# Two-layer encoder step on one core: the second layer's projection finishes block by block, with the sample's loads and first steps inside it

## The reference, cut to what matters

```
p = rmsnorm(x) @ w_in[l]      # -> mixer a | b | c | cross q | gate
even l: o = chunk-band softmax attention
odd  l: o, S = HGRN2 recurrence, then rmsnorm per head
y = concat(o, cross_attn(q_x, mem_k, mem_v)) * silu(gate);  x = x + y @ w_out[l]
```

```
A = cumsum(log_f)
o     = sum_s (q_t . exp(A_t - A_s) k_s) i_s  +  (q * exp(A)) @ S
S_new = exp(a_last) * S + (k * exp(a_last - A))^T @ i
```

## Time and profile before

| what | value |
|---|---|
| median of three runs | 2802.57 us (2802.24 to 2803.62) |
| the profiled execution: its own time | 2802.87 us |
| its span, first to last instruction | 2800.9 us |
| busy share of PE, PEld, DVE, ACT, POOL | 95%, 81%, 40%, 34%, 9% |
| mean granted TensorE clock | 0.973 |
| DMA | 273.21 MB, mean 98 GB/s |

### The profile page before, as it was taken

One profiled execution on the slowest core, in us unless ns is written; L12 is line 12 of the kernel. 1 busy time (PEld: TensorE's weight loads), 2 busy tenths in 40 slices (PEclk: granted clock), 3 DMA queues, 4 the chain that ended last, 5 costly groups with the idle time before them and its releaser, 6 DMA issues. The chain is left out here.

```text
span 2800.9 us, 45370 instructions
## 1 busy us (share of the span) xinstructions
PE 2651.8 (95%) x17253; PEld 2259.0 (81%) x17253; DVE 1111.9 (40%) x2432; ACT 957.4 (34%) x2314; POOL 265.5 (9%) x516
## 2 busy tenths in 40 slices
PE   7999999999669999999999999999998599999997
PEld 4899999999646777777778999999997488888886
DVE  5211111022145555555545112211122477777774
ACT  5111111111144555554545122111111545554553
POOL 2000000000002111111111000000001111111111
PEclk9999999999789999999999999999999799999999
DMA  6321212111593222221335223212112633333331
GB/s 226 141 77 64 74 66 72 69 63 63 119 263 115 71 63 77 71 84 55 95 106 143 78 89 125 99 63 78 63 62 92 221 100 95 95 104 111 95 95 59
DMA packets 271920, 273.21 MB, mean 98 GB/s; under 512 B 13808, under 2 KB 228904, under 8 KB 271764
## 3 DMA queue, kind: packets, MB, share of 16 engines
q1 hardware_dynamic: 258168, 221.43, 25.4%
q0 software_dynamic: 11936, 44.96, 4.6%
q10 hardware_dynamic: 1660, 4.75, 0.4%
HBM read 175.64 MB, written 100.18 MB: 98 GB/s over the span
## 5 line engine op out<-in xcount | busy, mean ns | idle before, releaser
L640 PE MATMUL pj_acc<-xh,pj_wh 128*128 128x384 f32 (+1 forms) x1120 | 400.4, 357 | 5.6 <-DVE pj_wl L610 5.6
L640 PE MATMUL pj_acc<-xl,pj_wh 128*128 128x384 f32 (+1 forms) x1120 | 400.6, 358 | 0.0
L640 PE MATMUL pj_acc<-xh,pj_wl 128*128 128x384 f32 (+1 forms) x1120 | 400.6, 358 | 0.0
L902 PE MATMUL pj_acc<-xl,pj_wh 128*128 128x384 f32 (+1 forms) x1040 | 371.1, 357 | 0.0
L902 PE MATMUL pj_acc<-xh,pj_wl 128*128 128x384 f32 (+1 forms) x1040 | 370.9, 357 | 0.0
L902 PE MATMUL pj_acc<-xh,pj_wh 128*128 128x384 f32 (+1 forms) x1040 | 370.5, 356 | 0.0
L640 PEld LDWEIGHTS pj_acc<-xh,pj_wh 128*128 128x128 f32 x1120 | 211.0, 188 | 24.0 <-DVE pj_wl L610 5.8
L640 PEld LDWEIGHTS pj_acc<-xh,pj_wl 128*128 128x128 f32 x1120 | 210.9, 188 | 18.3
L640 PEld LDWEIGHTS pj_acc<-xl,pj_wh 128*128 128x128 f32 x1120 | 210.9, 188 | 17.8
L1993 ACT COPY pb_pt<-pb_TP 128x384 f32<-128x384 f32 (+2 forms) x272 | 107.0, 393 | 312.1 <-PE pb_TP L1725 237.0
L902 PEld LDWEIGHTS pj_acc<-xh,pj_wl 128*128 128x128 f32 x1040 | 195.2, 188 | 16.8
(11 more groups left out here) (310 smaller groups left out, 4402.3 us busy)
## 6 DMA issues: line engine op xcount, KB each, us to landing
proj<-pj_stg SPq DMA_DIRECT2D x168, 192.0 KB, 1.9
proj<-pj_stg SPq DMA_DIRECT2D x112, 256.0 KB, 2.0
pj_wraw<-in_w_in_dram POOLq DMA_DIRECT2D x26, 1024.0 KB, 6.1
hg_x<-x_mid SPq DMA_DIRECT2D x17, 512.0 KB, 3.5
out_dram<-hg_x POOLq DMA_DIRECT2D x17, 512.0 KB, 3.0
bg_x<-in_x_prompt_dram SPq DMA_DIRECT2D x16, 512.0 KB, 4.5
pb_gate<-proj SPq DMA_DIRECT2D x16, 512.0 KB, 5.0
pb_x<-in_x_prompt_dram SPq DMA_DIRECT2D x16, 512.0 KB, 3.4
```

The lines of the kernel that those rows point to most:

```text
L640: ins = nc.tensor.matmul(acc[b][:, 0:n], w[p][:, k], x[:, k, at:at + n], start=(k == 0 and x is xh and w is wh), stop=(k == KD - 1 and x i ...
L902: ins = nc.tensor.matmul(acc[b][:, 0:n], w[p][:, k], x[:, k, at:at + n], start=(k == 0 and x is xh and w is wh), stop=(k == KD - 1 and x i ...
```

## The change

**norm_project.** Groups 26 and 27 are taken out of the loop. They are computed as a pair, block by block: block 0 of both, then block 1 of both, and so on. So block 0 of the tokens is no longer needed when a fifth of this tail is over. The tokens now lie in one buffer per block (`xh[b]`, `xl[b]`) instead of one for all. Tiles of the sample are placed over the first of these buffers: after the second store of the tail SP issues the loads of q, f, k, the values, the cross queries and the memory keys; after the fourth the memory values. The first product and the four steps (DVE and ACT parts) come between the tail's blocks. The section no longer ends with a wait for the stores; these waits stand in `sample_mix`, before the first state is stored (SP) and before `o_s` is written (DVE).

```diff
                     sweep(sp, lo, hi, 1, body)
-                for b in range(NBLK):
-                    sp.wait_ge(s_st[b], 16 * NG)
-                    sp.wait_ge(s_st2[b], 16 * MG)
+                tok = slice(SEQ, NTOK)
+                mk, mv = (c[l].rearrange("b (t p) h d -> p (b t) (h d)", p=P) for c in (cache_mem_k, cache_mem_v))
+
+                def load_sample():
+                    sp.wait_ge(s_st[NBLK - 1], 16 * GG)
+                    sp.wait_ge(s_st2[NBLK - 1], 16 * MG)
+                    for buf, src, s_in in ((samp.q, proj[GQ:GQ + MG, :, tok], samp.s_ld), (samp.f, proj[GK:GK + MG, :, tok], samp.s_ld),
+                                           (samp.k, kgate[:, :, tok], samp.s_ld), (samp.iT, proj[GV:GV + MG, :, tok], samp.s_li)):
+                        sp.dma_start(buf.rearrange("p (h n) -> p h n", n=P), src.rearrange("g p n -> p g n")).then_inc(s_in, 16)
+                    sp.dma_start(samp.xq[:], proj[GX:GX + 2, :, tok].rearrange("g p n -> p g n")).then_inc(samp.s_lx, 16)
+                    for i in range(2):
+                        sp.dma_start(samp.raw[:, SB * i:SB * (i + 1)], mk[:, SB * i:SB * (i + 1)]).then_inc(samp.s_lk[i], 16)
+                for n in range(2 * NBLK):
+                    c, (at, w) = pair_block(n)
+                    sp.wait_ge(s_stage, LASTS + n + 1)
+                    sp.dma_start(proj[TAIL + c][:, at:at + w], stage[n % NBLK][:, 0:w]).then_inc(s_st[n % NBLK], 16)
+                    if n == 1:
+                        load_sample()
+                    if n == 3:
+                        sp.dma_start(samp.vals[:], mv).then_inc(samp.s_lvals, 16)
...
+                gain(NG - 1, 1)
+                rest(NG - 1, 1)
+                sigs = NBLK * (seen + TAIL - GG)
+                for n in range(2 * NBLK):
+                    _, (_, w) = pair_block(n)
+                    mine = stage[n % NBLK][:, 0:w]
+                    dve.wait_ge(s_sig, sigs + n + 1)
+                    nc.vector.tensor_tensor(mine, acc[n % NBLK][:, 0:w], mine, ALU.mult).then_inc(s_stage, 1)
+                    if n == 5:
+                        samp.product(nc, dve)
+                        samp.step(nc, dve, 1)
+                    if n == 6:
+                        samp.step(nc, dve, 2)
+                        samp.step(nc, dve, 3)
+                    if n == 7:
+                        samp.step(nc, dve, 4)
...
+                sweep(pe, 2, TAIL, 2, body)
+                for n in range(2 * NBLK):
+                    c, (_, w) = pair_block(n)
+                    b, bank = n // 2, n % NBLK
+                    if b == 0:
+                        pe.wait_ge(s_wl, TAIL + c + 1)
+                    pe.wait_ge(s_stage, LASTS + n - NBLK + 1)
+                    for k in range(KD):
+                        for wx, x in ((wh, xh), (wl, xh), (wh, xl)):
+                            ins = nc.tensor.matmul(acc[bank][:, 0:w], wx[c][:, k], x[b][:, k],
+                                                   start=(k == 0 and x is xh and wx is wh), stop=(k == KD - 1 and x is xl))
+                    ins.then_inc(s_mm, 1)
```

```diff
-                for r in range(KD):
-                    if r == OWN:
-                        sp.wait_ge(s_lv, LEVELS)
-                        sp.wait_ge(s_st, LEVELS - 1)
-                    sp.dma_start(wraw[r], v["w_out"][l, r * P:(r + 1) * P]).then_inc(s_lw[r], 16)
+
+                def load_row(r):
+                    sp.dma_start(wraw[r], v["w_out"][l, ROWS[r] * P:(ROWS[r] + 1) * P]).then_inc(s_lw[r], 16)
+                for r in range(OWN):
+                    load_row(r)
+                sp.wait_ge(s_xt, HX)
+                load_row(OWN)
+                load_row(OWN + 1)
+                for b in range(NBLK):
+                    sp.wait_ge(samp.s_store[b], 16 * NG)
+                    sp.wait_ge(samp.s_store2[b], 16 * MG)
                 for h in range(MG):
                     sp.wait_ge(s_new, h + 1)
                     sp.dma_start(v["b_state_sample"][0, :, h].rearrange("b k v -> k b v"), st[:, :, h]).then_inc(s_out, 16)
+                    if h == 2:
+                        sp.wait_ge(s_wl, 1)
+                        load_row(KD - 1)
...
                     link(nc.gpsimd.memset(z[:], 0.0))
+                pool.wait_ge(c_dve, 2)
+                nc.gpsimd.tensor_copy(offs[:].rearrange("p (two n) -> p two n", two=2), par[:].unsqueeze(2).to_broadcast([P, 2, 256])
```

```diff
                 turn(2)
                 turn(3)
                 sums(0)
+                output(2)
+                values(0)
                 sums(1)
-                values(0)
+                output(3)
                 values(1)
-                output(2)
                 sums(2)
-                output(3)
+                output(4)
                 values(2)
                 sums(3)
-                output(4)
+                output(5)
                 values(3)
                 sums(4)
-                output(5)
...
                 def update(h):
-                    dve.wait_ge(s_dec, h + 1)
+
                     dve.wait_ge(s_kv, h + 1)
-                    mine = st[:, :, h].rearrange("p (qd two) n -> p qd two n", two=2)
-                    nc.vector.tensor_tensor(mine, mine, sums_of(h).rearrange("p qd (two n) -> p qd two n", two=2), ALU.add
-                                            ).then_inc(s_new, 1)
...
+                    if h % 2 == 0:
+                        dve.wait_ge(s_dec, h // 2 + 1)
+                        mine = st[:, :, h].rearrange("p (qd two) n -> p qd two n", two=2)
+                        nc.vector.tensor_tensor(mine, mine, sums_of(h).rearrange("p qd (two n) -> p qd two n", two=2), ALU.add
+                                                ).then_inc(s_new, 1)
+                        return
+                    dve.wait_ge(s_o, h + 1)
+                    for b in range(SB):
+                        ins = nc.vector.scalar_tensor_tensor(out=st[:, b, h], in0=st[:, b, h], scalar=tm[16][:, h * SB + b:h * SB + b + 1],
+                                                             in1=sums_of(h)[:, b // 2, b % 2 * P:(b % 2 + 1) * P],
+                                                             op0=ALU.mult, op1=ALU.add)
+                    ins.then_inc(s_new, 1)
...
+                spread_queries(0)
+                spread_queries(1)
+                dve.wait_ge(s_ka, 2)
+                spread_keys(0)
+                spread_keys(1)
+                dve.wait_ge(s_offs, 1)
                 for u in range(HX):
                     least(u)
-                dve.wait_ge(c_pool, masked(LEVELS - 1) + 2)
-                dve.wait_ge(s_st, LEVELS - 1)
-                dve.wait_ge(s_ca, LEVELS - 1)
-                dve.wait_ge(s_ka, 2)
-                spread(0)
-                spread(1)
                 for h in range(MG):
+                    if h + 2 < MG:
+                        spread_queries(h + 2)
                     update(h)
                     if h + 2 < MG:
-                        spread(h + 2)
+                        spread_keys(h + 2)
...
                 probs(2)
                 probs(3)
-                for h in range(1, MG):
-                    decay(h)
-                for h in range(MG):
+                decay(2)
+                for r in range(2):
+                    weights_high(r)
+                for h in range(4):
                     square(h)
+                decay(4)
+                square(4)
+                square(5)
+                for r in range(2, KD):
+                    weights_high(r)
```

333 lines of the change are left out of this document (172 added, 161 removed).

## The result

The changed kernel takes 2784.22 us (median of six runs, 2782.25 to 2788.41). The kernel before, run beside it six times, has a median of 2803.10; the ratio is 0.9918, its 95% interval 0.9892 to 0.9944. The forecast was 2787.2, which is 0.9945 of 2802.57. The time lies just inside the forecast's own range of 2783.9 to 2789.8. As a ratio to the kernel before it lies outside: that range is 0.9933 to 0.9954. The gain was 3 us larger than forecast. The profiled execution took 2783.93 us, its span is 2782.0, 18.9 less than before.

The account below looks back on a forecast made before the run. PE was taken as nearly always busy except around 2150 to 2240 us. Gains of 9.35 + 1.2 + 5.2 = 15.7 us from 2802.87 gave 2787.2 us, range 2783.9 to 2789.8.

Parts of the forecast that it names:

- The first gap: PE's idle time between projection and sample: no wait for stores or loads, PE starts 9.35 us earlier.
- From the first transpose to the scores: Sample's first stage: 16.66 us becomes 15.5, 1.2 us less, with ends of 13.8 and 16.6.
- The clock: First transpose to scores: one fall of PE's clock behind the shorter gap, 1.7 us lost.
- The idle time: First transpose to scores: PE's 1.7 us idle kept, as PE still waits for ACT's copies of the keys.
- From the scores to the means: Second half of the sample: queries, `sums(1)`, the end and the clock together take 5.2 us off 35.07.
- PE's new order: Scores to means: `sums(1)` wait gone, -1.54; values and sums moved behind the last output, -2.07; longer end, +1.4.
- From the means to the next section: Stage of DVE's eight low parts: stays at 13.2 us, gain zero; the last row's load has 6.1 us.
- The projection's tail: Groups 26 and 27: group 27's weights, needed one block after group 26 begins, fit by 0.9 us; zero cost.
- Odd updates dear: Rival, scores to means: odd updates take 4.5 us each, 5.6 us in all, 2792.8; chance 0.12.
- A new wait: Rival: PE waits 3.6 us for group 27's weights (2790.8) or DVE 4.3 for the last row (2791.5); together 0.10.
- Start not earlier: Rival, section change: POOL's preparation holds PE's levels until about 2165.5, only the second half gains, 2797 or more; chance 0.05.
- Loads ahead of stores: Rival, projection's tail: 3.8 MB of loads delay the third store, the projection stands 53 us, 2840; chance 0.05.

Follow-up runs that it names:

- b1_warm: The kernel before, with 48 unused identity transposes ahead of PE's first wait in the sample's section; 2807.5 us against 2802.14, ratio 1.0016.
- x4: The changed kernel with PE's outputs, sums and values in the order of before, the rest as after; 2785.03 us, ratio to before 0.9947.
- x6: The changed kernel with four low parts of the weights made earlier on DVE and two high parts earlier on ACT; 2783.54 us, ratio to before 0.9917.
- x1: The changed kernel with SP again waiting for all stores at the end of the projection's section; 2789.12 us, ratio to before 0.9954.

## Why the prediction was right or wrong

**The first gap: right.** Forecast 9.35, measured 9.52. Nothing waits for a store or a load any more. The tail paid nothing: the eight copies and thirteen DVE instructions lie between the sigmoids, and the last projection product ends at 2152.77, before at 2153.37.

**From the first transpose to the scores: this step failed.** The forecast was 13.8 + 1.7 = 15.5 us, with 13.8 as its lower end. Measured: 12.92 with no fall and 14.55 with one, so the forecast was too high in either case. Two errors, of which each is a term of the sum.
- *The clock*, 1.63 us: charged in full as one fall (1.7, and that size is right: 14.55 - 12.92), while in the first profiled execution there was none. The prediction had said that the trace cannot decide it, and then took one of the two cases for the forecast. It is a matter of the execution: six falls in eight.
- *The idle time*, 0.7 us: "which I keep". Before, PE waited 1.46 and 0.24 us for ACT's copies of the keys; after, 0.24, and 0.72 ahead of the scores, which the trace puts down to no engine. The copies are not faster (0.59 us each in both traces), but in the new order a level of products stands between the first pairs of key transposes, and ACT has no steps to do in between; which of the two did it was not tried apart. Keeping the idle time also set the lower end too high: 13.8 instead of 12.9. By b1_warm the error is larger than the 0.7 us show: the 13.8 stood for the old lists at the full clock, and these take 14.70, since PE then waits 2.12 us for ACT. So the new lists gained 1.78 us here, which the prediction put at nothing; against this, it took the clock's share in the stage before for 2.8 us, where b1_warm shows 1.96. The two errors partly cancel in 13.8.

The rest of the difference, 0.2 us, is within what the reading of a mean clock of 0.83 gives: PE's work at full clock is 11.99 us, where 14.9 - 2.8 = 12.1 was worked out.

**From the scores to the means: right in sum, 5.29 against 5.2, and in part by luck.** Most of the parts come out as rows. `output(0)`: 2.11 forecast, 2.27 when put back. `sums(1)`: the wait of 1.54 is gone. The end: from PE's last output (2189.64 + 1.95 = 2191.59) to the means 6.36 us, forecast 6.2. Two parts need a correction. The odd update takes 2.15 us and not 1.7; it was priced after a copy. The 0.6 us that the range allows upwards for the update is a term that no run shows; the runs showed 2.15 - 1.7 = 0.45 us more. And the clock's fall in `values` was counted half; it was absent, worth 3.85 - 2.41 = 1.44 us. What failed is the reason behind the sum: the forecast gave PE's new order 1.54 + 2.07 - 1.4 = 2.2 us, and x4 gives the same stage with the old order (29.49). Moving the outputs forward only exchanged the wait of `sums(1)` for that of `sums(5)` and a longer end. In the old order the gain of x4 over before, 35.07 - 29.49 = 5.58 us, is 2.11 for the queries, 1.44 for the clock in `values` and 4.76 - 2.85 = 1.91 at the end, from the lists of ACT and DVE. The prediction's term for PE's order thus had nearly the size of a gain that comes from elsewhere.

**From the means to the next section: nearly right**, -0.29 against 0. The low parts take what they took: the last ends at 2210.07. The section's change behind it takes 1.40 us instead of 1.04. SP's list shows a likely reason:

```profile
2201.84 0.35 SPq L1101 DMA_DIRECT2D sm_w<-in_w_out_dram  x1
2202.24 4.07 SPq L1112 DMA_DIRECT2D out_dram<-sm_state  x3
```

The state's last three stores stand behind the wait for the first low part, although the fourth state was ready at 2189.48 + 2.15 = 2191.63. They are issued until 2206.31 (the last from 2203.3 on) and take 5.0 to 6.9 us to land, so until about 2210.2, and SP's list ends with a wait for them. With the low parts early (x6) the change takes 2211.62 - 2210.53 = 1.09. That the stores do it was not tried by itself.

**The projection's tail: right**, no wait for group 27's weights. ACT's sigmoids around the tail's beginning and the loads among the stores:

```profile
2106.01 0.49 ACT L883 ACTIVATE pj_stg<-pj_acc 128x384 f32<-128x384 f32 x1 [3.67 <-PE pj_acc L1020]
2108.26 1.05 ACT L848 CAST pj_wh<-pj_wg 128x1024 fp32r<-128x1024 f32 x1 [1.75 <-DVE pj_wg L914]
2111.49 0.60 ACT L895 ACTIVATE pj_stg<-pj_acc 128x512 f32<-128x512 f32 x1 [2.18 <-PE pj_acc L1033]
2116.93 0.60 ACT L895 ACTIVATE pj_stg<-pj_acc 128x512 f32<-128x512 f32 x1 [4.84 <-PE pj_acc L1033]
```

```profile
2118.73 1.08 SPq L819 DMA_DIRECT2D sm_in<-proj  x2
...
2122.96 2.14 SPq L822 DMA_DIRECT2D sm_raw<-in_cache_mem_k_dram  x2
2125.14 4.38 SPq L826 DMA_DIRECT2D proj<-pj_stg  x2
```

The sigmoids come 5.44 us apart, as the blocks do, and the ten blocks take 46.8 us, from the sigmoid at 2106.01 to the last at 2152.80.

**The rivals.** *Odd updates dear* fell: 2.15 us, half of the 4.5. *A new wait* fell in the tail. For the last row ACT did wait, which the prediction had named as a sign of being wrong, but it cost nothing: ACT was done at 2205.72 + 1.15 = 2206.87, and DVE took the row up at 2208.79 without a wait.

```profile
2205.72 1.15 ACT L1408 ACTIVATE woh<-sm_w,g_hgrn 128x1024 fp32r<-128x1024 f32 x1 [6.87 <-DMA sm_w<-in_w_out_dram]
```

*Start not earlier* fell. *Loads ahead of stores* fell: the third store goes out at 2125.14, long before its tile is needed again.

## What to carry to other kernels

A gap between two sections costs its length and may cost the clock's price behind it, and the second was a matter of the execution here: forecast it as two cases with a chance each, 1.6 us apart behind 2.48 us of idle time (2.9 behind the 4.16 us of x1), not as one value. Eight or twelve unused transposes at the end of the section went with a clock that stayed at 1.00 (four executions of four), and cost nothing; twenty cost 0.56 us. Ask of a stage with a low clock what PE would wait for at the full one: warmed, the stage before gave back 1.96 us and not 2.8. And before a wait is removed by another order, look at which wait the order leaves last: here one of 1.46 us was exchanged for one of 1.47, and undoing the exchange took 0.29 us off.
